# Scores of an attention in four PSUM banks instead of two, and head norms taken between the weight slots of a projection

## What is computed

```python
qa, ka, va, qd, kd, vd, qm = split(rms(x) @ w_in)       # 4096 columns in all
qa, ka, qd, kd, qm = rms over each head of 64, times a gain
out_na  = neighbourhood attention, 8 heads               # scores + bias, softmax, times va
out_mem = attention over a memory, 4 heads               # km, vm come from another input
out_dil = 4 heads x 3 dilation groups, one softmax over the three groups
x = x + concat(out_na, out_dil, out_mem) @ w_out
x = x + moe(rms(x))                                      # 32 experts, all their weights are read
```

## Time and profile before

| what | value |
|---|---|
| runs | 2530.44, 2533.19, 2534.39 us, median 2533.19 us |
| profiled execution, its own time | 2535.62 us |
| its span, first to last instruction | 2533.8 us |
| TensorE busy | 2095.9 us, 83% |
| VectorE, ScalarE, GpSimd busy | 53%, 33%, 25% |
| granted TensorE clock, mean | 0.931 of full speed |
| HBM traffic | 363 GB/s over the span |

### The profile page before, as it was taken

How to read it: one execution, slowest core, us unless ns; L and a number is a source line. 1 busy time by engine, 2 the same in 40 slices (tenths; PEclk the granted TensorE clock), 3 DMA queues, 4 the chain that set the end, 5 groups by cost and what they waited for, 6 DMA issues and landing times.

```text
span 2533.8 us, 24529 instructions
## 1 busy us (share of the span) xinstructions
PE 2095.9 (83%) x8090; PEld 1057.2 (42%) x8090; DVE 1340.5 (53%) x3184; ACT 845.8 (33%) x2245; POOL 640.5 (25%) x601
## 2 busy tenths in 40 slices
PE   5997978888799889799889878887799976666765
PEld 1554543345265356255447323332474542222221
DVE  2875787666556976566976577764204420111110
ACT  1213144434344834344844435443103410000000
POOL 1001044433333433333333444443100300000000
PEclk9996989999999999999999999999899987878888
DMA  8792689999999999999999999999742149999997
GB/s 334 298 377 88 267 355 422 421 421 420 417 397 421 397 404 422 421 404 421 381 396 412 421 421 421 408 422 421 288 149 83 65 166 427 428 429 429 428 429 332
DMA packets 107448, 915.94 MB, mean 361 GB/s; under 512 B 12454, under 2 KB 12740, under 8 KB 15876
## 3 DMA queue, kind: packets, MB, share of 16 engines
q0 software_dynamic: 76800, 549.70, 53.2%
q1 hardware_dynamic: 30532, 364.82, 34.8%
HBM read 913.37 MB, written 6.06 MB: 363 GB/s over the span
## 4 chain that ended last, share of the span: by engine, by line
PE 40%; DMA 36%; DVE 14%; ACT 6%; issue 3%; POOL 1%; SPq 0%; DVEq 0%; POOLq 0%; ACTq 0%
DMA arena<-in_peer_uv_dram,arena 19%; PE summed L1085 15%; DMA arena<-in_moe_pieces_dram 15%; PE gp L1157 5%; DVE y L2232 4%; PE gp L873 3%; PE gp L888 3%; DVE h L2041 2%; DMA arena<-in_w_slots_dram 2%; PE gp L1153 2%; PE gp L1417 2%; ACT arena L1667 1%; POOL arena L819 1%; PE summed L986 1%; PE scores L959 1%
## 5 line engine op out<-in xcount | busy, mean ns | idle before, releaser
L1085 PE MATMUL summed<-arena 128*128 128x512 f32 x2048 | 1000.4, 624 | 204.9 <-ACT arena L1667 182.0
L2232 DVE CUSTOM_DVE_ANT_0 y<-arena,h 128x1024 f32<-128x1024 f32 x512 | 627.4, 1225 | 400.7 <-DMA arena<-in_peer_uv_dram,arena 348.4
L819 POOL DMA_INDIRECT arena<-in_peer_uv_dram,arena x512 | 580.9, 1135 | 927.8 <-PE summed L1085 817.6
L1085 PEld LDWEIGHTS summed<-arena 128*128 128x128 f32 x2048 | 370.6, 195 | 747.8 <-ACT arena L1667 395.8
L1661 ACT ACTIVATE arena<-arena 128x1 f32<-128x1 f32 x512 | 102.6, 200 | 517.1 <-DVE arena L2232 516.5
L1417 PE MATMUL gp<-arena,mod 128*32 128x512 f32 x1024 | 168.4, 794 | 112.8 <-DMA arena<-in_moe_pieces_dram 111.6
L1667 ACT ACTIVATE arena<-cst,arena 128x128 f32<-128x128 f32 x512 | 205.5, 401 | 16.7
L2579 DVE TENSOR_TENSOR mod<-mod,gp 128x512 f32<-128x512 f32 x8 | 5.5, 688 | 385.8 <-ACT mod L1892 385.8
L1664 ACT ACTIVATE arena<-arena 128x1 f32<-128x1 f32 x512 | 150.8, 294 | 19.9 <-DVE arena L2221 3.3
L888 PE MATMUL gp<-hT,arena 128*128 128x256 f32 x608 | 132.6, 380 | 3.0 <-DMA arena<-in_w_slots_dram 2.3
L873 PE MATMUL gp<-arena,hT 128*128 128x512 f32 x288 | 129.7, 611 | 6.1 <-DMA arena<-in_w_slots_dram 5.0
(11 more groups left out here) (397 smaller groups left out, 2022.3 us busy)
## 6 DMA issues: line engine op xcount, KB each, us to landing
arena<-in_moe_pieces_dram SPq DMA_DIRECT2D x96, 2048.0 KB, 25.6
arena<-in_w_slots_dram SPq DMA_DIRECT2D x47, 2048.0 KB, 10.4
mod<-in_w_parts_dram SPq DMA_DIRECT2D x29, 1024.0 KB
arena<-in_w_parts_dram SPq DMA_DIRECT2D x29, 1024.0 KB
arena<-in_peer_uv_dram,arena POOLq DMA_INDIRECT x512
t_rep<-t_rows POOLq DMA_DIRECT2D x1, 3066.0 KB, 14.2
arena<-t_rep POOLq DMA_DIRECT2D x1, 2304.0 KB, 11.0
na_rep<-na_rows POOLq DMA_DIRECT2D x1, 1778.0 KB, 8.1
```

Of the source, the lines that this page charges most:

```text
L819: pool.indirect_dma_start(rowbuf[b], None, a["peer_uv"].rearrange("l n d -> (l n) d"), bass.IndirectOffsetOnAxis(ap=idx[:, col(n):col(n) + ...
L1085: mm = pe.matmul(op[:, b, :], diag[:, n % DIAGS, :], rowbuf[n % ROWS][:, D + b * 512:D + (b + 1) * 512], start=n % SLOTS == 0, stop=n % SL ...
L2232: v.tensor_tensor_reduce(y[:, t, :], rowbuf[n % ROWS][:, 0:D], h[:, t, :], 1.0, 0.0, ALU.mult, ALU.add, dots[:, c:c + 1]).then_inc(udot, 1)
```

## The change

Four things change.

1. `scores` uses four banks, the two of `sp_` and the two of `gp`, and waits for the read of segment j-4 instead of j-2, in both attentions. Before each attention TensorE now waits until ScalarE has emptied `gp`.
2. The slots of block 2 are ordered with the values last: five column slots, then the mixed slot with its columns first, then the two value slots.
3. TensorE runs `project_and_norm`: after slot 1 the sums of pairs 0 and 1, and so on, two sums per step, and from slot 3 on two spreads per step; the last two value slots are taken a group at a time. ScalarE runs `move_and_norm` with the squares and roots between its copies. VectorE takes each reciprocal when its bank is first needed, and no longer waits for the whole projection.
4. `keep_clock` leaves block 2.

```diff
+    slots.append(("in2", view(*w, 3584), [("cols", 256, 20), ("rows2", 0, ("zn", 1024))]))
+    rows("in2", w, 1024, ("zn", 0))
     rows("in2", w, 3072, ("zn", 512))
-    slots.append(("in2", view(*w, 3584), [("rows2", 0, ("zn", 1024)), ("cols", 256, 20)]))
...
+        def score_bank(j):
+            return (sp_, gp)[j // 2 % 2][:, j % 2, :]
...
+            def head_sum(stage_name, i):
+                b, j = divmod(i, 4)
+                pe.wait_ge(qk_sq, qk_base[stage_name] + i + 1)
+                pe.matmul(norm_bank(b)[32 * j:32 * (j + 1), :], blk[:, 48:80], work[:, (i % 2) * 512:(i % 2) * 512 + 512],
+                          start=True, stop=True).then_inc(qk_sum, 1)
+            def head_spread(stage_name, i):
+                b, j = divmod(i, 4)
+                if j == 0:
+                    pe.wait_ge(qk_inv, qk_bank[stage_name] + b + 1)
+                if i >= 2:
+                    pe.wait_ge(qk_done, qk_base[stage_name] + i - 1)
...
+            def project_and_norm():
+                steps = [(0, None, (), ()), (1, None, (0, 1), ()), (2, None, (2, 3), ()), (3, None, (4, 5), (0, 1)),
+                         (4, None, (6, 7), (2, 3)), (5, None, (8, 9), (4, 5)), (6, 0, (10, 11), (6, 7)), (6, 1, (), (8, 9)),
+                         (7, 0, (), (10, 11)), (7, 1, (), ())]
+                for m, tile, sums, spreads in steps:
+                    project("in2", slice(m, m + 1), tile=tile)
+                    for i in sums:
+                        head_sum("block2", i)
+                    for i in spreads:
+                        head_spread("block2", i)
...
-                    if j >= 2:
-                        pe.wait_ge(s_read, b0 + j - 1)
+                    if j >= 4:
+                        pe.wait_ge(s_read, b0 + j - 3)
...
-            project("in2")
-            head_sums("block2")
+            project_and_norm()
             pe.wait_ge(qk_done, qk_base["block2"] + len(QK["block2"]))
+            pe.wait_ge(gemm_moved, last_group["in2"])
             attention("block2")
...
+            def move_and_norm():
+                steps = [(0, None, (0, 1), None), (1, None, (2, 3), None), (2, None, (4, 5), 0), (3, None, (6, 7), None),
+                         (4, None, (8, 9), 1), (5, None, (10, 11), None), (6, 0, (), 2), (6, 1, (), None), (7, None, (), None)]
+                for m, tile, squares, bank in steps:
+                    move("in2", slice(m, m + 1), tile=tile)
+                    if squares:
+                        act.wait_ge(gemm_moved, group_end(phase_slots["in2"][m]))
+                    for i in squares:
+                        head_square("block2", i)
+                    if bank is not None:
+                        head_root("block2", bank)
...
-            v.wait_ge(gemm_moved, last_group["in2"])
             head_norms("block2")
```

More of the change, by code:

```diff
@@ L155, in weight_stream @@
     cols("in2", w, 512, 4)
-    rows("in2", w, 1024, ("zn", 0))
     cols("in2", w, 1536, 8)
@@ L923, in hT_ready @@
                 pe.wait_ge(turn_moved, turned[0])
-            def head_sums(stage_name):
[L926 to L945, removed]
@@ new lines, in head_sum @@
+            def head_sum(stage_name, i):
[9 more added lines that the diff above has]
+                    pe.wait_ge(qk_done, qk_base[stage_name] + i - 1)
+                for half in range(2):
+                    r = 32 * j + 16 * half
+                    mm = pe.matmul(tp[64 * half:64 * (half + 1), i % 2, :], ident[:, r:r + 1].to_broadcast([P, 64]),
+                                   norm_scale(b), start=True, stop=True)
+                mm.then_inc(qk_spread, 1)
@@ new lines, in head_sums @@
+            def head_sums(stage_name):
+                for i in range(len(QK[stage_name])):
+                    head_sum(stage_name, i)
+                keep_clock("in0", 3)
+                for i in range(len(QK[stage_name])):
+                    head_spread(stage_name, i)
+            def project_and_norm():
[8 more added lines that the diff above has]
+                        head_spread("block2", i)
@@ L955, in scores @@
                     sg = segs[j]
-                    if j >= 2:
-                        pe.wait_ge(s_read, b0 + j - 1)
+                    if j >= 4:
+                        pe.wait_ge(s_read, b0 + j - 3)
                     for t in range(T):
-                        mm = pe.matmul(sp_[:, j % 2, t * S:t * S + sg["keys"][t]], sg["q"][:, t * P:(t + 1) * P],
+                        mm = pe.matmul(score_bank(j)[:, t * S:t * S + sg["keys"][t]], sg["q"][:, t * P:(t + 1) * P],
                                        sg["k"][:, 0:sg["keys"][t]], start=True, stop=True)
@@ L1308, in _ @@
             turn(y, 1)
+            pe.wait_ge(gemm_moved, group_end(vec_slots[13]))
             attention("moba")
@@ L1551, in norm, with head_square, head_root @@
                 act.activation(small[:, 62:64], small[:, 60:62], ACT.Sqrt).then_inc(rootd, 1)
-            def head_norms(stage_name):
[L1554 to L1565, removed]
+            def head_square(stage_name, i):
+                n0 = qk_base[stage_name]
+                if i >= 2:
+                    act.wait_ge(qk_sum, n0 + i - 1)
+                act.activation(work[:, (i % 2) * 512:(i % 2) * 512 + 512], zt2(QK[stage_name][i][0]), ACT.Square).then_inc(qk_sq, 1)
+            def head_root(stage_name, b):
+                act.wait_ge(qk_sum, qk_base[stage_name] + 4 * b + 4)
+                act.activation(norm_scale(b), norm_bank(b), ACT.Sqrt, scale=1.0 / 64, bias=eps[:, 0:1]).then_inc(qk_root, 1)
+            def head_norms(stage_name):
+                for i in range(len(QK[stage_name])):
+                    head_square(stage_name, i)
+                    if i % 4 == 3:
+                        head_root(stage_name, i // 4)
+            def move_and_norm():
[9 more added lines that the diff above has]
+                        head_root("block2", bank)
             def attention(stage_name):
@@ L1865, in _ @@
             move_turned_rows(1)
-            move("in2")
-            head_norms("block2")
+            move_and_norm()
             attention("block2")
@@ L1971, in head_norms @@
                 b0 = qk_bank[stage_name]
-                for b in range(len(q) // 4):
-                    v.wait_ge(qk_root, b0 + b + 1)
-                    v.reciprocal(norm_scale(b), norm_scale(b)).then_inc(qk_inv, 1)
                 for i, (c, g) in enumerate(q):
+                    if i % 4 == 0:
+                        b = i // 4
+                        v.wait_ge(qk_root, b0 + b + 1)
+                        v.reciprocal(norm_scale(b), norm_scale(b)).then_inc(qk_inv, 1)
                     v.wait_ge(qk_spread, n0 + i + 1)
@@ L1993, in attention @@
                             dst = logit(stage_name, sg, j, t)
-                            sc = sp_[:, j % 2, t * S:t * S + sg["keys"][t]]
+                            sc = score_bank(j)[:, t * S:t * S + sg["keys"][t]]
                             if sg["bias"][0] == "alibi":
```

## The result

The kernel after the change took 2517.67 us (median of 4 runs, 2514.93 to 2520.62), the kernel before 2532.88 in the same session (4 runs, 2530.44 to 2534.39): ratio 0.9940, 95% interval 0.9923 to 0.9957. The forecast was 2516.8 (2511 to 2526).

What follows compares the result with a forecast made beforehand. Head norms and attention, 1923 to 2016 us, were taken to bound the kernel, holding back the expert stage. Gains 9.4 + 7.0 = 16.4 us take 2535.62 to 2519.2, or 2516.8 as the runs' median; range 2511 to 2526.

Steps and rivals of the forecast that it cites:

- What bounds it: Between 1923 and 2016 us, head norms and attention: each us saved there should come off the end in full.
- Part 1, the norms: Block 2's head norms laid between input slots: 28.1 us leave the chain, 18.7 are added, gain 9.4 us.
- the third bank's chain: Last norms bank: root, multiplications and reciprocal, 5.6 us in a row, fit their cover by 3.
- The prediction's estimate by that rule: Tiling-mode switches among the norms' matmuls: 20 at 0.16 us, 18.8 in place of 18.0, gain 8.6.
- Part 2, the attention: Four score banks in block 2's attention: 8.2 us at full clock, 7.0 after one dip, bounds 3 and 9.
- Fill: Start of block 2's attention: first turn and first values 3.1 us earlier; 1.2 if the clock dips as before.
- Steady state: Rounds of scores 10 to 20 in block 2's attention shorten, by 5.1 us in all.
- I keep 1.2 us for one dip: Block 2's attention: 1.2 us allowed for one fall to the lower clock, taking 8.2 to 7.0.
- the rival on the other side: Clock stays low through block 2's attention, making it about 24 us longer: 2548; decides from about 33 us low; chance 0.03.
- Part 3, moba: Four score banks in the moba attention: 0 us, with 1 either way for where the clock changes.
- The sum: Whole kernel: 9.4 + 7.0 = 16.4 us gained, forecast median 2516.8.
- the round does not shorten: Block 2's attention: copies wait for values of the same round, only the norms' gain is left: 2523.8; chance 0.12.

Runs made afterwards that it cites:

- copy_early: Kernel after the change, with ScalarE's copy of a turned segment one step earlier in block 2's attention; 2527.72 us, ratio 0.9984 to the kernel before.
- filler_fit: Kernel after the change, with 1, 2 and 1 useless matmuls ahead of block 2's turns of segments 0, 2 and 12; 2518.60 us, ratio 0.9954.
- before_again: The kernel before, unchanged, run once more for a second profile; 2530.26 us (1 run).
- three_three: Kernel after the change, with block 2's six attention banks split three for scores, three for turned weights; 2519.48 us, ratio 0.9958 to the kernel before.
- moba_two: Kernel after the change, with two score banks in moba and four in block 2; 2520.27 us, ratio 0.9951 to the kernel before.
- norms_only: Kernel after the change, with the scores of both attentions back in two banks; 2521.73 us, ratio 0.9953 to the kernel before.
- banks_only: Kernel before, with four score banks in both attentions, norms and slot order unchanged; 2529.10 us, ratio 0.9983 to the kernel before.
- filler: Kernel after the change, with 2, 5 and 3 useless matmuls ahead of block 2's turns of segments 0, 2 and 12; 2523.57 us, ratio 0.9964.
- two_fill: Kernel after the change, with 1, 2 and 1 useless matmuls in block 2 and two score banks in both attentions; 2525.23 us (1 run).
- three_fill: Kernel after the change, with block 2's 3 + 3 bank split and 1, 2 and 1 useless matmuls; 2520.44 us, ratio 0.9955 to the kernel before.

## Why the prediction was right, and where it was not

**What bounds it:** right. The us saved between the slots and the attention's end came off the end: what follows took 517.1 us (517.7 before).

**Part 1, the norms: 8.7 for a forecast 9.4.** The mechanism was right; the size was off by one missing term. The pieces were a little cheaper than forecast, 6 x 0.98 + 6 x 1.87 = 17.1 for 18.0. What was missing is that the projection itself grew. The groups by form of the kernel after:

```profile
L892 PE MATMUL gp<-hT,arena 128*128 128x256 f32 x352 | 77.3, 380 | 0.7 <-ACT hT L1568 0.7
L877 PE MATMUL gp<-arena,hT 128*128 128x512 f32 x64 | 28.5, 599 | 0.0
```

They were 76.6 and 27.8: 1.4 more busy time for the same matmuls. The chain of waits of the kernel before has the same slots without a cut:

```profile
1854.77 41.44 PE gp L888 x192
1896.21 13.73 PE gp L873 x32
```

That is 13.81 for a slot of L888, which takes 14.01 between two insertions, and 6.87 for half a slot of L873, which takes 7.06 to 7.08. So each of the eight places where the stream is cut costs it about 0.2, 1.6 in all, and 28.1 - (17.1 + 1.6 + 0.7) = 8.7. No sum or spread waited, and the third bank's chain fitted, as worked out.

The Trainium skill (TensorEngine Tiling (Array Packing), Key Properties) says that a change of the tiling mode drains the engine. The prediction's estimate by that rule was 18.8 for the norms' matmuls and the switches together, a gain of 8.6; the trace agrees, with 17.1 + 1.6 = 18.7 and 8.7, though it does not tell the drain from another cost of a cut.

**Part 2, the attention: 1.6 for a forecast 7.0.** This is the part that failed, in its sizes, at three places.
- *Fill, 3.1 forecast.* The first turn was at 5.23 as forecast, but the values of segment 2 were only 17.20 - 14.81 = 2.4 earlier at full clock. The step named the copy that "does not move" and did not follow it to its next reader, the turn of segment 2, which needs the bank that it empties. copy_early shows it: with that copy 1.4 us earlier, the values of segment 2 are 17.20 - 13.37 = 3.8 earlier.
- *Steady state, 5.1 forecast.* Of the rounds named there, at full clock (filler_fit) that of scores 10 fell from 4.34 to 3.95, 12 from 4.34 to 3.97, 14 from 4.33 to 3.11, 16 stayed at 5.56, 18 fell from 4.34 to 3.95 and 20 from 7.42 to 5.83: 4.0, and the next lost 0.3: 3.7. But 1.3 of that is the dip of before, not the banks: in before_again, at full clock, the round of 20 took 46.01 - 40.22 = 5.79 with two banks, so four banks took nothing off it, and by like clock the rounds gave 2.3 in all. The mechanism was right (two bases side by side in 1.07); the round of 10 has two bases and still came at 3.95, because its turn stands behind ScalarE's copy too; in three_three, with a third bank for the turned weights, it took 19.59 - 16.32 = 3.27.
- *"I keep 1.2 us for one dip".* It cost 4.5: at segment 16 the kernel after stands at 51.25 and filler_fit at 46.73. 2.4 + 3.7 - 4.5 = 1.6, which is what was measured. moba_two, with the same code here, lost 48.00 - 46.73 = 1.3 to its dips up to that point: the term is one that moves.

So the largest miss is in the steady state: 2.3 at full clock, where the forecast had 5.1, of which 0.8 stood for the dip. The rounds of 10, 16 and 20 were taken to shorten and were held by other waits, for ScalarE's copy and for GpSimd's divides. The fill can't be separated in this way, as every profile with two banks has a dip in it.

The Trainium skill (TensorE: Matmul & The Clock Gate, A second HAM failure mode: psum-queue depth-cycling) tells of a kernel that swings between the two clock levels as it idles for moments between groups; the traces agree in kind, with two or three dips in most of the attentions here. The prediction weighed this as the rival on the other side. Its condition was not met: 13.7 us at the lower level, as before, and 20.5 at most in any run, for the 33 from which it decides.

**Part 3, moba:** 0 as forecast for the banks; the clock moved it by 3.2 from one execution to another, where the forecast allowed 1.

**The sum.** By the stages 8.7 + 1.6 = 10.3, which would be 2522.6. The medians differ by 15.2 (10.9 to 19.5 by the interval), and norms_only and banks_only by 11.9 and 4.3, with intervals of 5 and 3 either way. The 5 us between the stages and the medians are not located. The intervals reach far enough for them to be noise: the same change measured again as moba_two gave 12.4, and the banks of block 2 gave 4.3 (banks_only) and 1.5 (moba_two against norms_only) in medians, for the forecast 7.0. A profile is one execution: moba alone varies by 3.2 and more, the untouched 1550 us by 8. That the forecast lay 0.9 from the median is then in part luck: two terms too large, and some 5 us that no stage of two profiles accounts for. The rival "the round does not shorten" (2523.8) had the nearer size for the attention and the wrong reason: the rounds did shorten.

**What stays open:** why three_three and filler_fit, with attentions 3 to 4 us shorter than that of the kernel after in their profiles, are not faster than it in their medians (2519.48 and 2518.60, ratios 0.9958 and 0.9954 for 0.9940, with intervals that overlap). Dips that fall otherwise in the timed runs would explain it, but no run here shows those. No version measured here beats the kernel after.

## What to carry to other kernels

When a serial wait in a software pipeline is taken away, follow every buffer of the same round to its next user: here the score banks handed the wait to the banks of the turned weights. One spare bank for each ring (3 + 3) took a further 0.7 us out of one round, but the whole kernel was not measurably faster for it. Cutting short waits for other engines out of a stretch bound by TensorE, by laying its small matmuls between large ones, came out as costed to within a us. In a stage with waits of 1 to 2 us the clock is a term of its own, as large as the gain: forecast it from the dips of before at their full length, read two attentions at the same time at the lower level or not at all, and take a second profile before you read one profile's dips as the kernel's.

## What the runs showed of the hardware

- The moba attention ran with no dip (19.41) or with 11 to 15 us at the lower level (22.5 to 24.7), with either number of banks; three of fourteen profiles had no dip.
- A dip of like length costs by where it falls: 3.4 us at the lower level cost the kernel after 1.6 by segment 2, and moba_two nothing, where TensorE was waiting for ScalarE meanwhile.
- In norms_only TensorE was busy for 129.29 of 130.07 us at clock 1.00, with a wait of 0.78 at their end; after 1.1 us of scores it waited 0.80, and the clock fell 0.4 us behind that. Short waits were enough there.
- Whether matmuls without use in the waits hold the clock is not shown: filler and filler_fit kept 1.00 for 55.6 and 52.4 us, and in two_fill and three_fill it had fallen before the first of them ran.
- A pair of sums to different groups of 32 columns takes 0.98 and two halves of 64 columns run side by side, 1.87 for eight instructions of 512 columns; each cut in the dense stream costs it about 0.2.
